# A two-layer decoder trunk on one core: GpSimd adds up the squares of an RMS norm, and TensorE sums 4 chunks of them instead of 16

## What is computed

```python
def _rmsnorm(x, g):
    xf = x.astype(jnp.float32)
    y = xf * lax.rsqrt(jnp.mean(xf * xf, axis=-1, keepdims=True) + EPS)
    return y.astype(x.dtype) * g

for l in range(DEPTH):                       # DEPTH = 2
    ...
    hn = _rmsnorm(x, norm1_g[l]) * (1 + sc1[:, None]) + sh1[:, None]
    m, ... = _token_mixers(hn, ...)          # ends with  mixed @ w_out[l]
    x = x + g1[:, None] * m
    hn = _rmsnorm(x, norm2_g[l]) * (1 + sc2[:, None]) + sh2[:, None]
    f, ... = _conv_ffn(hn, ...)              # ends with  (...) @ w_down
    x = x + g2[:, None] * f
y = _rmsnorm(x, final_g)
```

## Time and profile before

| | |
|---|---|
| runs | 3686.79, 3692.32, 3693.62 us; median 3692.32 |
| the profiled execution | 3687.15 us, span 3685.4 us |
| mean granted TensorE clock | 0.962 |
| TensorE busy | 3470.7 us (94% of the span), 24056 matmul instructions |
| VectorE, ScalarE, GpSimd busy | 1927.1 (52%), 1396.0 (38%), 97.5 us (3%) |
| ones-matmuls on SQ | 160 instructions, median 432 ns |
| squares on ScalarE | 40 instructions, median 722 ns |

### The profile page before, as it was taken

One profiled execution on the slowest core, in us unless ns is written; L12 is line 12 of the kernel. 1 busy time (PEld: TensorE's weight loads), 2 busy tenths in 40 slices (PEclk: granted clock), 3 DMA queues, 4 the chain that ended last, 5 costly groups with the idle time before them and its releaser, 6 DMA issues.

```text
span 3685.4 us, 58409 instructions
## 1 busy us (share of the span) xinstructions
PE 3470.7 (94%) x24056; PEld 3149.5 (85%) x24056; DVE 1927.1 (52%) x3745; ACT 1396.0 (38%) x2432; POOL 97.5 (3%) x159
## 2 busy tenths in 40 slices
PE   5899998898999999999999999898889999999998
PEld 1678876687888888888888999877889999999997
DVE  1344443556655445544554555537576646664664
ACT  0333332423433233333333544334254434443443
POOL 1000010001000000000000000100000000000000
PEclk7899998998999999999999999999999999999999
DMA  9676665743677667777775444434334454444443
GB/s 321 220 216 209 200 206 165 239 150 92 217 221 230 219 223 222 224 228 223 224 222 161 113 124 121 115 91 150 107 114 149 149 153 147 153 149 149 150 141 106
DMA packets 484122, 646.40 MB, mean 175 GB/s; under 512 B 25742, under 2 KB 427514, under 8 KB 483528
## 3 DMA queue, kind: packets, MB, share of 16 engines
q1 hardware_dynamic: 473472, 608.51, 52.7%
q0 software_dynamic: 10384, 34.16, 3.3%
HBM read 628.09 MB, written 14.49 MB: 174 GB/s over the span
## 4 chain that ended last, share of the span: by engine, by line
PE 85%; DMA 5%; DVE 4%; ACT 2%; issue 2%; DVEq 1%; ACTq 0%; POOL 0%; SPq 0%; POOLq 0%
PE PS L1310 83%; DMA RAW<-in_w_ada 2%; PE PS L1314 2%; DMA RAW<-in_w_in 1%; DVE WLO L886 1%; DMA RAW<-in_ffn_w_up 1%; PE PS L1327 1%; ACT WHI L601 1%; DVEq L877 1%; DMA RAW<-in_ffn_w_down 1%; DVE CY L1116 0%; DMA RAW<-in_w_out 0%; DVEq L900 0%; DVE TMP L1095 0%; DVEq L880 0%
## 5 line engine op out<-in xcount | busy, mean ns | idle before, releaser
L886 DVE TENSOR_TENSOR WLO<-RAW,WHI 128x512 fp32r<-128x512 f32 x1584 | 1044.0, 689 | 1217.6 <-ACT WHI L601 1201.7
L601 ACT ACTIVATE WHI<-RAW 128x512 fp32r<-128x512 f32 x1584 | 955.5, 627 | 1619.9 <-PE PS L1310 787.7
L1310 PE MATMUL PS<-HH,WHI 128*128 128x320 f32 (+1 forms) x4384 | 1405.4, 321 | 89.7 <-DVE WLO L886 55.9
L1310 PE MATMUL PS<-HL,WHI 128*128 128x320 f32 (+1 forms) x4384 | 1371.4, 313 | 0.0
L1310 PE MATMUL PS<-HH,WLO 128*128 128x320 f32 (+1 forms) x4384 | 1370.6, 313 | 0.0
L1310 PEld LDWEIGHTS PS<-HH,WHI 128*128 128x128 f32 (+1 forms) x4384 | 832.4, 190 | 187.4 <-issue 120.5
L1310 PEld LDWEIGHTS PS<-HL,WHI 128*128 128x128 f32 (+1 forms) x4384 | 833.0, 190 | 0.0
L1310 PEld LDWEIGHTS PS<-HH,WLO 128*128 128x128 f32 (+1 forms) x4384 | 831.7, 190 | 0.0
L1310 PE MATMUL PS<-MH,WHI 128*128 128x320 f32 x1920 | 616.0, 321 | 46.4 <-DVEq L900 27.0
L1310 PE MATMUL PS<-ML,WHI 128*128 128x320 f32 x1920 | 601.1, 313 | 0.0
L1310 PE MATMUL PS<-MH,WLO 128*128 128x320 f32 x1920 | 600.7, 313 | 0.0
(11 more groups left out here) (266 smaller groups left out, 1762.7 us busy)
## 6 DMA issues: line engine op xcount, KB each, us to landing
RAW<-in_w_ada SPq DMA_DIRECT2D x384, 512.0 KB, 4.5
RAW<-in_ffn_w_up SPq DMA_DIRECT2D x352, 512.0 KB, 3.6
RAW<-in_ffn_w_down SPq DMA_DIRECT2D x176, 512.0 KB, 3.8
RAW<-in_w_in SPq DMA_DIRECT2D x160, 512.0 KB, 3.9
RAW<-in_w_out SPq DMA_DIRECT2D x64, 512.0 KB, 3.7
RAW<-in_w_in SPq DMA_DIRECT2D x32, 384.0 KB, 4.1
ST<-in_state_gla POOLq DMA_DIRECT2D x8, 576.0 KB, 7.7
out_gla_s<-ST POOLq DMA_DIRECT2D x8, 576.0 KB, 4.2
```

What stands on the lines that cost most here:

```text
L601: A(WHI[:, g % 4], RAW[:, u % 4, c % 4:c % 4 + 2, :], ACT.Copy).then_inc(hi_ready, 1)
L886: V.tensor_tensor(WLO[:, g % 4], RAW[:, u % 4, c % 4:c % 4 + 2, :], WHI[:, g % 4].bitcast(f32), ALU.subtract).then_inc(split_ready, 1)
L1310: return nc.tensor.matmul(out, w, x, start=start, stop=stop)
```

## The change

In each of the five places GpSimd now adds the squares of panels 1 to 6 into those of panel 0, as they appear: six `tensor_tensor` adds of 128x640, each waiting for `sq_ready`, with a drain between them. The last of them signals `sum_ready`. TensorE then runs ones-matmuls over four chunks: the two of the sums, and, behind a wait for the last square, the two of panel 7. These stand all at the end of the stage (`mean_square`), where pairs 0 to 5 stood between the panels; at the start they stand behind unit 58. In GpSimd's program the sums of a place stand behind the retention stores and, for the second norm of a layer, behind the stores of the conv state; `params(1)` comes behind the sums of the first, and the hold on `mix_ready` ahead of it goes.

```diff
+            def sum_squares(n):
+
+                for i in range(1, 7):
+                    pool.wait_ge(sq_ready, 8 * n + i + 1)
+                    op = nc.gpsimd.tensor_tensor(SQ[:, 0:2], SQ[:, 0:2], SQ[:, 2 * i:2 * i + 2], ALU.add)
+                    if i < 6:
+                        nc.gpsimd.drain()
+                op.then_inc(sum_ready, 1)
...
             params(0)
+            sum_squares(0)
             for l in range(DEPTH):
...
+                sum_squares(2 * l + 1)
                 if l + 1 < DEPTH:
-                    hold(mix_ready, l * 3 + 3)
                     params(l + 1)
                 hold(xo_rows, l + 1)
                 pool.dma_start(O["fconv_s"][l].rearrange("b k (g n) -> (b k g) n", g=8), OUTF[:]).then_inc(rows_out, 16)
                 pool.dma_start(O["fconv_p"][l].rearrange("b k (g n) -> (b k g) n", g=8), OUTP[:]).then_inc(rows_out, 16)
+                sum_squares(2 * l + 2)
...
-            def ones_sum(name, l, n, first, end):
-                b = bank(name, l)
-                if first == 0:
-                    begin(name, l)
-                for i in range(first, end):
-                    pe.wait_ge(sq_ready, 8 * n + i + 1)
-                    for k in (2 * i, 2 * i + 1):
-                        op = mm(b[:, 0:T], ONES, SQ[:, k, :], k == 0, k == KC - 1)
-                if end == 8:
-                    op.then_inc(job_done, 1)
+            def mean_square(name, l, n):
+
+                b = begin(name, l)
+                pe.wait_ge(sum_ready, n + 1)
+                for k in range(2):
+                    mm(b[:, 0:T], ONES, SQ[:, k, :], k == 0, False)
+                pe.wait_ge(sq_ready, 8 * n + 8)
+                for k in (KC - 2, KC - 1):
+                    op = mm(b[:, 0:T], ONES, SQ[:, k, :], False, k == KC - 1)
+                op.then_inc(job_done, 1)
...
-                    elif q == 3:
-                        ones_sum("ss2", l, 2 * l + 1, 0, 2)
-                    else:
-                        ones_sum("ss2", l, 2 * l + 1, q - 2, q - 1)
-                ones_sum("ss2", l, 2 * l + 1, 6, 8)
+                mean_square("ss2", l, 2 * l + 1)
...
-                            elif q == 5:
-                                ones_sum("ss1", l + 1, 2 * l + 2, 0, 4)
-                            elif q > 5:
-                                ones_sum("ss1", l + 1, 2 * l + 2, q - 2, q - 1)
-                ones_sum("ss1", l + 1, 2 * l + 2, 6, 8)
+                mean_square("ss1", l + 1, 2 * l + 2)
...
-                elif i < 23:
-                    ones_sum("ss1", 0, 0, 2 * i - 38, 2 * i - 36)
+                elif i == 23:
+                    mean_square("ss1", 0, 0)
```

More of the change, by code:

```diff
@@ L351, in build @@
         sq_ready = sem("sq_ready")
+        sum_ready = sem("sum_ready")
         ms_ready = sem("ms_ready")
```

## The result

The changed kernel takes 3671.73 us (median of 5 runs, 3660.09 to 3676.36) against 3692.32 of the kernel before in the same session (5 runs, 3685.53 to 3696.41): a ratio of 0.9941, 95% interval [0.9918, 0.9963], some 21 us faster. A second comparison, in a later session, gave 3666.58 against 3678.87, 0.9967 [0.9954, 0.998], 12 us. The profiled execution, 3676.36 us with a span of 3674.5, is the longest of its five, while that of the kernel before (3687.15) lies near the short end of its runs; so the two traces are only 10.9 us apart, and stages have to be compared one by one.

What follows compares the result with a forecast made beforehand. TensorE was taken to bound outR and down2, busy every microsecond. Terms: 21.5 + 1.0 - 1.5 - 4.2 = 16.8 us gained, giving 3675.5 from the median 3692.32; forecast 3675, range 3664 to 3686.

Steps and rivals of the forecast that it cites:

- The gain in the stages: Two ends each of outR and down2: ones-matmuls leaving TensorE save 5.38 or 5.39 us a place, 21.5 us gained.
- VectorE's cover in `outR`: In outR VectorE needs 2.6 us of a 3.52 us panel; added waits up to 0.9 us a panel cost nothing.
- first rival: outR gets no faster because VectorE, held by each add, becomes the bound; only down2 gains, 6.1 us, 3686; chance 6%.
- The add: One 128x640 two-input add on GpSimd takes 1.3 us, with ends of 0.61 and 2.6 us.
- The serial tail: At the four stage ends the sixth add holds the update of X, delaying square 8: 1.5 us lost together.
- hidden, just: At the outR end, matmuls over the sums run T + 2.9 to T + 3.75, before the last pair at T + 3.95.
- T: The moment at which the last weight matmul of a stage's panel 7 has been issued.
- the opposite case: If add_back's instructions reading PSUM and X were held too: about 0.9 us more a place, 3.6 us, left to the range.
- The clock: TensorE's silence at stage ends halves its clock in two places of four, 2.1 us each: 4.2 us lost (0 to 8.4).
- third rival: Clock falls in all four places and the add takes 2.6 us: 7.4 us gained, 3685; chance 8%.
- The start: At the start (ss1 of layer 0), where DMA sets the pace, 1.0 us is won (0 to 1.5).
- The moved loads: 17 parameter loads for layer 1, now behind the sixth add of outR, cost nothing; some 35 us left for landing.

Runs made afterwards that it cites:

- long adds: Changed kernel with each GpSimd add behind two more of its size into a scratch tile, each with a drain: 3701.58 us.
- one-input run: Changed kernel with the product for the last update of X kept in PSUM, so that update reads one operand from SBUF: 3672.62 us.
- busy tail: Changed kernel with all six adds, TensorE also summing panels 5 and 6 with the result overwritten: 3654.8 us, 0.9932 of the kernel before.
- no adds: Changed kernel with GpSimd waiting and signalling but adding nothing, the mean taken over four chunks only: 3657.05 us, 0.9941 of the kernel before.
- filler of 22: Five adds, plus 22 constant matmuls on TensorE through the norm at three places: 3654.86 us, 0.9917 of the kernel before.
- five adds: Changed kernel with GpSimd adding panels 1 to 5 only, TensorE taking the pairs of panels 6 and 7: 3650.47 us, 0.9922 of the kernel before.

## Why the prediction was right, and where it was not

**The gain in the stages: right.** 21.5 us forecast, 22.0 measured (21.9 in the second trace). Three places agree to 0.02 us with 5.38 and 5.39; `outR` of layer 1 gave 0.5 more. That 0.5 is luck: it lies in the first panel, 6.11 us before and 5.62 in the changed kernel, which has no ones-matmuls in any kernel and takes 5.6 to 6.5 us among all runs. The other panels of that stage give 5.37.

**VectorE's cover in `outR`: right.** The prediction gave VectorE 2.6 us of a panel's 3.52 and 0.9 of room. Without adds VectorE is busy 7.98 us in three panels (2.7 a panel); with them 9.52 (3.2). So the holds ate 0.5 of the 0.9 us a panel, and some 0.35 was left. The long adds show what comes when that is gone: the first rival's mechanism, which is real, and needed an add three times as long.

**The add: 1.57 us (median) against the 1.3 taken**, within the bounds of 0.61 and 2.6. The Trainium skill's "GPSIMD Engine Reference" (Elementwise, side-by-side cycle accounting), from which 1.4 was estimated, came closer than the cast's row. The drains were as free as forecast.

**The serial tail: right size, wrong mechanism.** 1.5 us forecast, 1.8 measured. But the prediction let the held update of X delay square 8 and the last pair, and called the two matmuls over the sums "hidden, just". The one-input run took away the hold, and the tails stayed. What delays the last pair is the step called hidden: the four instructions over the sums start when the add is done, and the last pair has to stand behind them. In the busy tail, with the clock up, they start at T + 3.1 and the last pair at T + 4.3 (last layer: T + 2.6 and T + 3.8), behind square 8's end, held or not, in each place (T + 4.0 to 4.1; last layer T + 3.5). The failing figures are the add's end, T + 2.85 forecast and T + 3.06 measured, and 0.84 us for those four instructions, which take 1.2 before the next can start. Nor does `outR` of layer 1 show the same tail as layer 0, as the prediction read it: its update of X starts at T + 3.01 before the change, too late to be held (0.29 us in the changed kernel). Place by place the busy tail grew by 0.41, 0.40, 0.05 and 0.92 us (both of layer 0, then `outR` and `down2` of layer 1), where 0.2, 0.2, 0.2 and 0.94 were forecast; that the sums agree so well is luck.

The Trainium skill's "SBUF — State Buffer" (Who interferes with whom) says that a VectorE instruction with at most one SBUF input, outside the modes that use both ports, doesn't contend with GpSimd. No row of before showed it; the one-input run does (0.29 us inside a running add), and so do the `add_back` instructions on PSUM and X in the long-adds run (0.86 us). The 3.6 us that the prediction kept for the opposite case fell away.

**The clock: the mis-sized term.** 4.2 us forecast, as two places of four at 2.1; measured 6.2, as four of four at 1.25 to 1.75. The frequency was too low, and the price too high, so the two errors partly made up for each other. The prediction had all eight instructions at half the clock. Where that came about, in the long adds, they took 4.60 us against 2.42 in the busy tail: 2.2 more, the price forecast. In the changed kernel they took 3.58, 3.98, 4.08 and 3.85, since only a part of them ran at half the clock. At the two ends of `outR` it fell behind their start (at about 905.0 against 903.92, and 2697.0 against 2696.83); at the two of `down2` it was down ahead of them, as forecast (2014.3 against 2014.48, 3649.3 against 3649.74); and at all but the first it rose again before they were done. So the third rival's first half came true (all four places), and its second half, an add of 2.6 us, didn't; without that its price is 22.5 - 6.2 - 1.8 = 14.5 us, still clear of the bound.

**The start: not confirmed.** 1.0 us forecast. The changed kernel shows 127.67 and 129.29 us against 129.59, but runs with the same start spread from 127.5 to 131.4.

**The moved loads: right.** They are issued from 903.72 on, 3.0 us behind T as forecast, and the last at 911.78; TensorE uses the first at 950.31, between other matmuls and without waiting. The norms take 7.86 to 7.87 us in every run, but for one of 8.01 in the one-input run.

**The sum.** 22.0 - 8.0 = 14.0 us on the touched path, against 21.5 - 1.5 - 4.2 = 15.8 forecast. The medians moved by 20.6 us in one session and 12.3 in the other; both lie around it, and the difference between sessions is of the size by which the untouched stages vary. The forecast's 3675 is 3.3 us from the median, though the tail was 2.3 us dearer than the two terms for it (8.0 against 5.7). That closeness is partly luck: the prediction had no term for the variation of untouched stages, which is larger.

## What to carry to other kernels

Work that moves from a bound engine to an idle one pays between the steps, where it has a whole step of time, and costs at the last step, where everyone waits: hand over all but the last items (here all but the last cost 8.0 us, and all but the last two nothing). Before taking work from TensorE at the end of a stage, list its new silences; here four of 2.5 to 3 us gave back 6.2 of 22 us through the clock. And where a hold is seen, take it away before charging for it: the instruction that is visibly longer wasn't the one on the path.

## What the runs showed of the hardware

- The clock can fall after TensorE has resumed: silent from 900.7 to 903.9, at work from 903.92, granted 0.98 in 904 to 905 and 0.50 from 905 on. Equal silences (1.60 and 0.73 us, no adds) brought it down at the end of `outR` of layer 0 and not at that of `down2`.
- Of two traces of a stage that no edit touches, the longer had the lower mean clock: the mixer of layer 1 took 636.1 us at 0.93 in the changed kernel and 628.1 at 0.95 with the filler of 22. Between executions of one kernel (five adds) the mixer of layer 0 took 731.9 and 744.6 us, at 0.95 and 0.94.
- GpSimd and VectorE hold each other both ways: the add of 891.68 that started beside a split subtraction took 1.88 us instead of 1.57, and pairs of split subtractions beside back-to-back adds took 3.98 us.
